# Chunks of an RWKV-7 recurrence on four quadrants of TensorE's array instead of two

## What is computed

```
def step(S, inp):                       # S: [head, value 64, key 64]
    sa = S @ kk_t
    S  = S * w_t - sa (kk_t * a_t)^T + v_t k_t^T
    y  = S @ r_t
```

## Time and profile before

| | us |
|---|---|
| median of 3 runs | 1501.95 (1501.89 to 1502.12) |
| the profiled execution | 1501.0 |
| its span, first to last instruction | 1499.2 |
| start of pair 0's slot | 130.0 |
| pairs 0 to 5, each | 61.9 |
| pair 6, pair 7 (to the turned state) | 63.55, 42.5 |

### The profile page before, as it was taken

One profiled execution on the slowest core, in us unless ns is written; L12 is line 12 of the kernel. 1 busy time (PEld: TensorE's weight loads), 2 busy tenths in 40 slices (PEclk: granted clock), 3 DMA queues, 4 the chain that ended last, 5 costly groups with the idle time before them and its releaser, 6 DMA issues. The chain is left out here.

```text
span 1499.2 us, 34641 instructions
## 1 busy us (share of the span) xinstructions
PE 1257.2 (84%) x15148; PEld 1140.8 (76%) x15148; DVE 718.3 (48%) x1101; ACT 483.7 (32%) x771; POOL 87.1 (6%) x145
## 2 busy tenths in 40 slices
PE   4777999999999998678599999526999999699953
PEld 1377888888888887565599999516999999699952
DVE  2334455555555544377233232284666666722226
ACT  0343333432434323322322222104544444322211
POOL 0002021120210202010000000000000000000000
PEclk9889999999999999785699999857999999899985
DMA  8131011010110100359623232312222222133221
GB/s 276 64 85 47 4 47 49 2 49 10 41 49 2 35 2 4 116 126 291 203 86 90 84 91 74 125 56 57 85 84 84 84 84 84 38 105 89 77 85 64
DMA packets 185345, 117.26 MB, mean 78 GB/s; under 512 B 6624, under 2 KB 177430, under 8 KB 184935
## 3 DMA queue, kind: packets, MB, share of 16 engines
q1 hardware_dynamic: 185233, 115.58, 26.3%
HBM read 108.40 MB, written 7.34 MB: 77 GB/s over the span
## 5 line engine op out<-in xcount | busy, mean ns | idle before, releaser
L199 PE MATMUL PJ<-Hh,Wh 128*128 128x260 f32 (+1 forms) x1088 | 244.9, 307 | 54.1 <-DVE Wl L1725 20.3
L199 PEld LDWEIGHTS PJ<-Hh,Wh 128*128 128x128 f32 x1088 | 173.7, 194 | 73.6 <-issue 32.2
L199 PE MATMUL PJ<-Hl,Wh 128*128 128x260 f32 (+1 forms) x1088 | 224.6, 289 | 0.0
L199 PE MATMUL PJ<-Hh,Wl 128*128 128x260 f32 (+1 forms) x1088 | 223.5, 287 | 0.0
L199 PEld LDWEIGHTS PJ<-Hl,Wh 128*128 128x128 f32 x1088 | 173.4, 194 | 0.0
L199 PEld LDWEIGHTS PJ<-Hh,Wl 128*128 128x128 f32 x1088 | 173.2, 193 | 0.0
L1725 DVE TENSOR_TENSOR Wl<-RAW,Wh 128x1024 fp32r<-128x1024 f32 (+1 forms) x68 | 80.8, 1194 | 100.8 <-ACT Wh L1665 96.2
L1665 ACT ACTIVATE Wh<-RAW 128x1024 fp32r<-128x1024 f32 (+1 forms) x68 | 70.1, 1036 | 111.0 <-PE PJ L199 103.4
L1745 DVE SCALAR_TENSOR_TENSOR ACC<-ACC,CP 128x512 f32<-128x512 f32 x88 | 66.0, 750 | 69.6 <-ACT ACC L1676 68.0
L1419 DVE TENSOR_TENSOR Wl<-RAW,Wh 128x1024 fp32r<-128x1024 f32 (+1 forms) x40 | 44.7, 1119 | 112.0 <-ACT Wh L1381 111.2
L199 PE MATMUL PJ<-SFh,Wh 128*128 128x260 f32 x352 | 71.9, 286 | 13.0 <-DVE Wl L1725 13.0
(11 more groups left out here) (312 smaller groups left out, 2446.2 us busy)
## 6 DMA issues: line engine op xcount, KB each, us to landing
RAW<-in_w_in_dram SPq DMA_DIRECT2D x46, 512.0 KB, 4.1
RAW<-in_ffn_up_dram SPq DMA_DIRECT2D x44, 512.0 KB, 3.8
RAW<-in_ada_w_dram SPq DMA_DIRECT2D x32, 512.0 KB, 6.0
RAW<-in_ffn_down_dram SPq DMA_DIRECT2D x16, 512.0 KB, 4.1
RAW<-in_ada_w_dram SPq DMA_DIRECT2D x2, 2048.0 KB, 11.3
ACC<-in_ada_w_dram SPq DMA_DIRECT2D x2, 2048.0 KB, 13.5
RAW<-in_w_branch_rwkv_dram SPq DMA_DIRECT2D x8, 512.0 KB, 4.1
RAW<-in_w_out_dram SPq DMA_DIRECT2D x8, 512.0 KB, 4.1
```

What stands on the lines that cost most here:

```text
L199: mm = pe.matmul(out[:, b, 0:nb[b]], w[:, slot, kw, :], x[:, kx, c0:c0 + nb[b]], start=first and w is Wh and x is xh, stop=last and w is Wl)
```

## The change

For every batch but level 0, the chunks are dealt to straight and crossed products in turn, each kind into a bank of its own, so that neighbouring products of a batch lie in all four quadrants. What a chunk's result is stored under follows from it: for odd chunks BP, MO, TI and W of head h lie in the other half (`bp`), XI and TT in the half that `b_at` names by level; KP, VT and AW go by `kq` and the partner chunk's place. Copies out of PSUM read two banks at a time (`pairs`), 256 columns of each.

With it come these changes of order and waits:
- The turns are three batches with one signal each: keys (32 products, once the first two masks are done), V and the odd chunks of ARI (24, after all four masks), and the even chunks of ARI (8, straight, moved into level 1 between L640 and L644). Level 0 waits for ACT's copies of both keys, `tr_ev` 5c + 2, in place of the first copy only.
- Level 0's TT comes from a new batch on PE (identity times MO), after ACT's copies of V and ARI, and a DVE copy that adds the identity, in place of L944.
- The copy of L630's result waits for DVE's TT copy of level 2, and level 3's TT batch for that copy.
- QM has one signal in place of two; the products that write QM's banks again (L675, L687) wait for both of its copies.
- One step of projection moves from the chunk loop (j = 3) to ahead of L687. Both columns of the mask are C_MN, and the copy of L630's result has no scale.

The core of the diff:

```diff
+            def kq(h, j):
+                return HH[1 - (h ^ j & 1)]
+            def bp(h, j):
+                return HH[h ^ j & 1]
+            def b_at(lv, h, j):
+                return HH[h ^ (lv & 1 & (j ^ j >> 1))]
+            def x_pos(lv, j):
+                return (j >> 1 & 1, (j >> 2) * 2 + (j & 1)) if lv % 2 else (j & 1, j >> 1)
+            def t_pos(lv, j):
+                return x_pos(1, j) if lv == 1 else ((j ^ j >> 1) & 1, j >> 1)
+            def flat(p):
+                return 4 * p[0] + p[1]
+            def pairs(c0, b0=0):
+                return BB[:, b0:b0 + 2, c0:c0 + 256].rearrange("p r (q t) -> p r q t", t=C)
+            def by_parity(m):
+                return m.rearrange("p (q r) t -> p r q t", r=2)
+            def by_type(m):
+                return m.rearrange("p (r q) t -> p r q t", r=2)
...
+                    pe.wait_ge(S("gram_ev"), 4 * c + 2)
+                    for j in range(NJ):
+                        at = C * (j // 2)
+                        for h in range(2):
+                            pe.matmul(B[j % 2][bp(h, j), at:at + C], BK[HH[h], j, 0, :], I2[HH[h], :], start=True, stop=True)
+                        for h in range(2):
+                            mm = pe.matmul(B[1 - j % 2][kq(h, j), 256 + at:256 + at + C], BK[HH[h], j, 1, :], I2[HH[h], :], start=True, stop=True)
+                    mm.then_inc(S("t_in"), 1)
...
+                    pe.wait_ge(S("mo0"), c + 1)
+                    pe.wait_ge(S("tr_ev"), 5 * c + 2)
+                    for j in range(NJ):
+                        for h in range(2):
+                            mm = pe.matmul(B[0][bp(h, j), j * C:(j + 1) * C], MO[bp(h, j), 0, j, :], I2[bp(h, j), :], start=True, stop=True)
+                    mm.then_inc(S("mm_x"), 1)
+                    pe.wait_ge(S("tr_ev"), 5 * c + 4)
+                    for j in (0, 2, 1, 3, 4, 6, 5, 7):
+                        r, q = x_pos(1, j)
+                        for h in range(2):
+                            mm = pe.matmul(B[2 + r][b_at(1, h, j), q * C:(q + 1) * C], I2[bp(h, j), :], MO[bp(h, j), 0, j, :], start=True, stop=True)
+                    mm.then_inc(S("mm_tt"), 1)
...
+                        for j in order:
+                            r, q = x_pos(lv, j)
+                            ti = j if lv == 1 else flat(x_pos(lv - 1, j))
                             for h in range(2):
-                                mm = pe.matmul(B[0][HH[h], j * C:(j + 1) * C], MO[HH[h], lv % 2, j, :],
-                                               I2[HH[h], :] if lv == 0 else TI[HH[h], j, :], start=True, stop=True)
+                                mm = pe.matmul(B[r][b_at(lv, h, j), q * C:(q + 1) * C], MO[bp(h, j), lv % 2, j, :], TI[bp(h, j), ti, :],
+                                               start=True, stop=True)
...
+                                    mm = pe.matmul(B[r][bp(h, j), 256 + q * C:256 + (q + 1) * C], TT[b_at(lv, h, j), flat(t_pos(lv, j)), :],
+                                                   XI[b_at(lv, h, j), flat((r, q)), :], start=True, stop=True)
...
+                            mm = pe.matmul(B[j % 2][bp(h, j), at:at + P], TT[HH[h], flat(t_pos(2, j)), :],
+                                           AW[HH[h], j ^ 1, :, :].rearrange("p s t -> p (s t)"), start=True, stop=True)
...
+                    dense(1)
+                    pe.wait_ge(S("mm_v"), 3 * c + 2)
...
-                        dense(1)
                         if j == 3 and nxt:
                             gate(c + 1)
+                        else:
+                            dense(1)
...
-                    act.wait_ge(S("t_in"), 4 * c + 1)
-                    act.activation(VT, bank8(0), ACT.Copy).then_inc(S("tr_ev"), 1)
+                    act.wait_ge(S("t_in"), 3 * c + 1)
+                    act.activation(by_parity(BP[:, :, 2, :]), pairs(0), ACT.Copy).then_inc(S("tr_ev"), 1)
+                    act.activation(by_parity(KP[:, :, 2, :]), pairs(256), ACT.Copy).then_inc(S("tr_ev"), 1)
...
+                            act.wait_ge(S("tt"), LEVELS * c + 3)
+                            act.activation(by_parity(AW[:, :, 1, :]), pairs(256, 2), ACT.Copy).then_inc(S("nv_ev"), 1)
...
-                        dve.tensor_tensor(XI, bank8(0), rows8(I2), ALU.add).then_inc(S("xi"), 1)
+                        dve.tensor_tensor(by_type(XI), pairs(0), eyes, ALU.add).then_inc(S("xi"), 1)
```

More of the change, by code:

```diff
@@ new lines, in slot @@
+                    mm.then_inc(S("mm_tt"), 1)
+                    if nxt:
+                        za(c + 1)
+                    for lv in range(1, LEVELS):
+                        order = sorted(range(NJ), key=lambda j: x_pos(lv, j)[::-1])
+                        pe.wait_ge(S("mo"), (LEVELS - 1) * c + lv)
+                        if lv == 1:
+                            pe.wait_ge(S("xi"), LEVELS * c + 1)
+                        else:
+                            pe.wait_ge(S("ti"), (LEVELS - 2) * c + lv - 1)
+                        for j in order:
+                            r, q = x_pos(lv, j)
+                            ti = j if lv == 1 else flat(x_pos(lv - 1, j))
@@ L625, in slot @@
                         dense(2)
+                        pe.wait_ge(S("xi"), LEVELS * c + lv + 1)
+                        pe.wait_ge(S("tt"), LEVELS * c + lv)
+                        if lv < LEVELS - 1:
+                            for j in order:
+                                r, q = x_pos(lv, j)
+                                for h in range(2):
+                                    mm = pe.matmul(B[r][bp(h, j), 256 + q * C:256 + (q + 1) * C], TT[b_at(lv, h, j), flat(t_pos(lv, j)), :],
+                                                   XI[b_at(lv, h, j), flat((r, q)), :], start=True, stop=True)
+                            mm.then_inc(S("mm_ti"), 1)
@@ L626, in slot @@
+                        if lv == 1:
+                            for j in range(0, NJ, 2):
+                                at = 256 + C * (j // 2)
+                                for h in range(2):
+                                    mm = pe.matmul(B[2][HH[h], at:at + C], ARI[HH[h], j, 0, :], I2[HH[h], :], start=True, stop=True)
+                            mm.then_inc(S("t_in"), 1)
                         if lv == 2:
-                            pe.wait_ge(S("tr_ev"), 4 * c + 4)
+                            pe.wait_ge(S("tr_ev"), 5 * c + 5)
@@ new lines, in slot @@
+                    mm.then_inc(S("mm_v"), 1)
+                    dense(1)
+                    pe.wait_ge(S("mm_v"), 3 * c + 2)
+                    for j in range(NJ):
+                        at = C * (j // 2)
+                        for h in range(2):
+                            mm = pe.matmul(B[2 + j % 2][HH[h], at:at + C], W[bp(h, j), j, 1, :], BP[bp(h, j), j, 1, :], start=False, stop=False)
+                    mm.then_inc(S("mm_v"), 1)
+                    pe.wait_ge(S("mm_v"), 3 * c + 3)
```

155 lines of the change are left out of this document (70 added, 85 removed).

## The result

| | before | after |
|---|---|---|
| median, runs | 1501.92 us, 4 (1500.52 to 1502.12) | 1441.93 us, 4 (1439.01 to 1444.1) |
| the profiled execution | 1501.0 | 1439.01 |
| its span | 1499.2 | 1437.2 |

The ratio is 0.9601, 95% interval 0.9582 to 0.962: faster by 60 us. The saving was under-estimated by a fifth (49.4 us forecast).

A forecast was written before the change was run, and what follows sets the result against it. PE's own work was taken to bound pairs 0 to 6. Gains of 6.5 us a pair gave 45.5, plus 5.5 in pair 7, less 1.6 for the clock: 49.4 us, so a 1452.5 us median, range 1440 to 1480.

The forecast's parts named there:

- The bound: Pairs 0 to 6: PE's own work sets the time, busy 59.7 of 61.9 us in a middle pair.
- Four quadrants at 64 columns: Spread 64-column batches: straight and crossed records overlap, 0.60 us if PE's queue was empty, 0.48 if full, instead of 0.93.
- 1. Gram to level 1: Gram to level 1's first product: 8.68 us becomes 8.2, with 0.5 idle before level 0; gain 0.5 a pair.
- 2. Level 1 to 3: Level 1 to level 3's start: seven batches save 2.3 to 3.2, moved turns cost 0.47; gain 2.2 a pair.
- 3. Level 3 to 4: Level 3 to 4: chain through ACT's TI copy already binds, only the first batch shrinks; gain 0.36, PE idle some 1.2 us.
- 4.: Level 4 to 5: three batches shorter; gain 1.2 us a pair.
- 5.: Level 5 to L665: two batches save 0.8, L658's saving brings nothing as L665 waits for W's copy; gain 0.8.
- 6.: L665 to the next pair: five batches save, QM wait costs 0.4, moved projection step about 0.3; gain 1.5.
- Pair 7: Last pair, no projections, chain of batch and copy: gain 5.5 us after 1 lost to the wait on QM.
- Half absorbed: Rival: longer copies or queue order make levels end on TI's copy; items 2, 4, 6 give half; 1470 to 1482, chance 0.19.
- No gain at 64 columns: Rival: 27 ns is a floor per record, so a small batch saves only 0.06 us; 1493, chance 0.08.
- slower: Rival: straight and crossed products in a batch take turns, only L665 gains; 0.75 us a pair lost, 1507.5, chance 0.05.

The follow-up runs named there:

- grouped run: Changed kernel, but in the recurrence's batches (except Gram products, level 0 and moved turns) all straight products come before the crossed ones; 1486.54 us, ratio 0.9903.
- Experiment 4: Changed kernel with ACT's square behind level 3's TI copy: 1442.28 us; then also level 3's projection step behind level 4's first batch: 1440.43 us.
- experiment 2: Changed kernel with only the W batch (L718, 128 columns) grouped, straight products first; 1441.55 us, ratio 0.9603.
- experiment 3: Changed kernel with the projection step ahead of L753 moved back into the chunk loop; 1441.03 us, ratio 0.9604.
- experiment 5: Changed kernel with W's batch one projection step earlier and W's copies ahead of R's shift and mix; 1448.48 us, ratio 0.9643.
- blocks of two: Changed kernel with batches ordered in turn as two chunks straight (8 records), two chunks crossed (8 records); 1451.33 us, ratio 0.9661.
- the run with the later step: Changed kernel with ACT's square behind level 3's TI copy and level 3's projection step behind level 4's first batch; 1440.43 us, ratio 0.9583.
- the run with the copy first: Changed kernel with only ACT's square of the next K moved behind level 3's copy of TI; 1442.28 us, ratio 0.9596.
- the last kernel: Changed kernel with later level-3 step, TI, YF and WK copies first, BV behind the masks, W's batch early, DVE's removal steps in the chunk loop; 1424.26 us.

## Why the prediction was right, and where it was off

**The bound.** Right. PE's own work set a pair's time, and 9.7 us of busy time less gave 7.4 us of pair.

**Four quadrants at 64 columns.** Right, and the grouped run shows it by itself. The Trainium skill's rule in "TensorE: Matmul & The Clock Gate", section "Part 3: Packing small matmuls", that a weight load overlaps running products only if its row group is another, would have left the batch at 1.15 us; 0.69 speaks against it for these fp32 products. **The size was off, in one term**: "a spread 64-column batch costs 32 x 19 = 0.60 us if PE's queue was empty before it". From first to last start it is 0.48 us, that is 15 ns a record, behind other work and behind a wait alike: the two batches at 260.79 and 266.37 (idle before it: 0.28) both last 0.69 to the last end. The 19 ns was read from two waits of L118 around 64 Gram records. That interval bounds the price of a hand-over from above, and the 15 ns between starts here show that it lies below; probably the queue was held back there by PE itself, at 27 ns a record. I took a bound for the price. The Trainium skill, "TensorE: Matmul & The Clock Gate", section "Back-to-back issue gap", names an issue floor of about 25 ns for products of 1 to 64 columns. The records here start 15 ns apart over four quadrants; a product, which is recorded twice, takes 30 ns, and one quadrant starts a record every 58 ns. So the floor, if it counts records, does not hold across quadrants; within one these runs don't reach it.

**Stage by stage**, pair 1 of after against pair 2 of before (in brackets the forecast). X1, X3, X4 and X5 are the first products of levels 1, 3, 4 and 5, QM that of the old L665:

| from, to | before | after | gain |
|---|---|---|---|
| start to X1 | 8.68 | 8.06 | 0.6 (0.5) |
| X1 to X3 | 13.82 | 11.23 | 2.6 (2.2) |
| X3 to X4 | 6.02 | 5.58 | 0.44 (0.36) |
| X4 to X5 | 6.56 | 5.19 | 1.4 (1.2) |
| X5 to QM | 8.82 | 7.91 | 0.9 (0.8) |
| QM to the next pair | 18.01 | 16.49 | 1.5 (1.5) |

1. Gram to level 1: right; PE waits 0.39 us for ACT's second key copy where 0.5 was forecast. All added pieces cost what they should.
2. Level 1 to 3: the 0.4 missing are the batch's size. The merged wait between NV's copy and TT never ends last. In pair 2 level 3 comes 0.3 us later (54.82 us for 54.46), but not for want of the cover that I called just enough: level 2's first product stands at 254.85, 13.68 us into the pair, where that of pair 1 stands at 13.67, with no idle time before it. The time goes inside the batch L703 of level 2 (258.11, 0.95 us for 0.65), to which the profile shows no wait. A like pause of 0.4 stands before L655 in pair 4.
3. Level 3 to 4: the amount of idle time was right (forecast 1.2, measured 0.88 + 0.28), its place half wrong. I followed ACT's order to the TI copy and took that for the last to come; the projection step between the batches waits for its bank, which DVE's mix of K reads. Experiment 4 shows both chains: taking the ACT square away gives 0.3, moving the step 0.8 in all.
4. Right but for the batch's size.
5. The gain is right but for the batch's size, and that W's batch gains nothing is shown by experiment 2. The place of the idle time is wrong in the same way as in level 3: of the 1.27 us, only 0.33 stand where W's copy is waited for, as much as before the change, and 0.94 at the projection step, whose bank DVE's mix of R reads. Both times I followed what the batch needs and not what the step of projection ahead of it needs.
6. The total was right by errors that cancel. L746 does not wait for QM (0.4 forecast), and the moved step costs some 0.05 (0.3 forecast). Against that the five batches save 1.6 us where I put 2.2 to 2.7: in the kernel of experiment 3, with the step back in the loop, it is 4.62 us from L665's successor to the loop's first product, against 6.20 before. For 0.4 us of what is missing the runs show the reason: four of them already ran in part beside a neighbour, as PE's timeline of the kernel before shows:

```profile
299.18 0.27 PE L671 MATMUL BB<-RAW,KP 64*64 64x64 f32 x2
299.28 0.28 PE L665 MATMUL BB<-BP,W 64*64 64x128 f32 x2
...
300.88 0.27 PE L680 MATMUL BB<-W,BP 64*64 64x64 f32 x2
300.92 0.28 PE L675 MATMUL BB<-KP,RAW 64*64 64x64 f32 x3
```

L671 (crossed) starts before L665 (straight) is done, L680 before L675 is; so the four batches from L665 on took 4.15 us (297.81 to 301.96, where the next product starts) and not the 4.5 that their records give one after the other (1.74 and three times 0.93). What already overlaps can't be saved again. The other 0.2 to 0.7 us are not split up further. The cover of QM's eviction is thin, as the forecast of 0 to 0.5 said: in experiment 5, with PE 1.9 us earlier, the wait was 1.2 us.

Pair 7 gained 6.5 us from its first Gram product to the copy of the turned state (42.96 to 36.48) for 5.5: again the missing wait for QM and the batch size.

**The sum.** Pairs 0 to 6 took 435.1 us before and 384.4 after: 50.7 for 45.5, of which 1.6 is the stretch at 1.2 GHz that pair 6 of before had and no pair of after. Pair 0 gained only 5.5: PE waits 2.1 us there for a DMA (1.7 before) and stands 1.2 us with no wait that the profile shows. With pair 7 the recurrence gives 57.2. The rest of the span, with the changed lines in none of it, took 5 us less in the profiled execution (891.1 to 886.1); in the variants above the same instructions took 886 to 890, with the stretches of lower clock in other places. Against the 1451.6 forecast for the profiled execution, its 1439.0 is 12.6 less: 3.6 from the pairs' work, 1.0 from pair 7, 1.6 from pair 6's stretch, 1.6 from one more such stretch that I added and that did not come, and 5.0 from the rest of the span. So a third of the miss is the recurrence's own work, most of it the size of the batch, and two thirds are the clock or stand outside the change (8.2 of 12.6 us), which the stages' working does not cover; this execution was also the fastest of its four, 2.9 us under their median.

**Rivals.** Half absorbed: excluded by the copies' unchanged durations and by the stage table. No gain at 64 columns, and slower: excluded by 0.69 us a batch. The grouped run sits where a kernel would that spreads quadrants but not neighbours.

## What to carry to other kernels

Small products in a row run side by side in full only if neighbours in program order use different quadrants; deal them out one by one (blocks of two cost 0.05 us a batch, grouping 0.3). Each kind had a bank of its own in every kernel made from the change, so whether it needs one is not shown. When PE work shrinks, list for each wait both what the batch needs and what the filler between batches needs: here the filler waited twice for a bank, and half of the idle time in level 3 could be had by issuing it one step later. A move that makes one engine earlier must be followed to the next engine's queue: W's batch earlier alone made the kernel 6 us slower by the medians; with DVE's steps reordered as well the pairs were the shortest of all.

## What the runs showed of the hardware

- PE starts matmul records of a second quadrant kind ahead of earlier ones of the first: in a grouped batch 16 straight records are issued first, and the crossed ones begin after 10 of them have started; in blocks of 8 records they begin after 2. Both times 6 earlier records were waiting, and the grouped batch of 128 columns (L723) gives the same 10 of 16: in these batches PE did not start a record of the other kind past more than 6 waiting ones.
- Four quadrants take a 64-column fp32 record each per 58 ns, all at once (32 records in 0.48 us from first to last start; the starts of a batch are 0, 7, 13, 20, 107, 113, 120, 127, 165 ns and so on); 128 columns take 109 ns in each. With four at work the cadence in one quadrant is the same as with two.
- Stretches of 3.4 us at 1.2 GHz (a window of before from 502.0 to 505.4 us has a granted clock of 0.50) stand in some pairs, right behind the 1.5-us wait for WK: in one pair of the kernel before, in two pairs each of the grouped run, of the blocks of two, of the run with the later step and of that with W early, in none of the kernel after. Each costs 1.6 us (55.25 against 53.64 above). They are not tied to that wait alone: the run with the copy first had one of 6.8 us in pair 0, the run in blocks of two and the last kernel one of 6.8 us in pair 7. No run here varied idle time alone, so what brings them on stays open. Single runs of one kernel differ by 1 to 8 us, and gains of 2 us in the pairs did not show in a median.
